# Sample attention that begins with the sliding branch, in a decoder step on one core

## What is computed

```python
o_cmp = softmax(q . kcmp) . vcmp                   # compressed blocks, 127 of them
idx   = top_k(importance of 33 blocks of 64, 16)   # 2048 past tokens and the new one
o_sel = softmax(q . k[idx blocks]) . v[idx blocks] # branch "sel", paged cache
o_win = softmax(q . k[last 512]) . v[last 512]     # branch "win", own cache
o     = g0 * o_cmp + g1 * o_sel + g2 * o_win
o_mem = softmax(qm . kmem) . vmem                  # branch "mem", 256 memory tokens
```

## Time and profile before

| | us |
|---|---|
| median of the runs | 1694.38 |
| the profiled execution, whole | 1689.1 |
| its span | 1687.2 |
| PE busy | 1472.1 (87%) |
| DVE busy | 880.0 (52%) |
| ACT busy | 374.7 (22%) |
| POOL busy | 82.0 (5%) |
| sample attention, within the span | 805 to 950 |

### The profile page before, as it was taken

The page is one execution under the profiler, slowest core; times in us unless marked ns, Lnnn a source line. Parts: engine busy times, 40 slices in busy tenths (PEclk is TensorE's granted clock), DMA queues, the critical chain, the costliest instruction groups (busy, mean ns, idle before and its releaser), DMA issues. The chain is left out here.

```text
span 1687.2 us, 27010 instructions
## 1 busy us (share of the span) xinstructions
PE 1472.1 (87%) x11343; PEld 1348.7 (80%) x11343; DVE 880.0 (52%) x1598; ACT 374.7 (22%) x874; POOL 82.0 (5%) x76
## 2 busy tenths in 40 slices
PE   6999899879878788988556567999989999999998
PEld 5778789879877677867344447999979999999998
DVE  3554257658434556654233264445654746555563
ACT  3543033223314344544122100010003101000000
POOL 0000001100011111110000000000000000000000
PEclk8999999989958798988678658999989999999999
DMA  9231125142401000000754342332341233233231
GB/s 342 87 131 59 50 79 179 51 175 79 132 10 51 0 1 1 1 1 8 302 204 156 97 149 77 92 96 77 99 164 38 75 101 100 79 97 99 75 101 51
DMA packets 115649, 159.03 MB, mean 94 GB/s; under 512 B 6040, under 2 KB 106840, under 8 KB 112779
## 3 DMA queue, kind: packets, MB, share of 16 engines
q1 hardware_dynamic: 111886, 122.76, 22.7%
q0 software_dynamic: 2304, 33.56, 4.9%
q10 hardware_dynamic: 1348, 1.12, 0.2%
HBM read 145.04 MB, written 16.66 MB: 96 GB/s over the span
## 5 line engine op out<-in xcount | busy, mean ns | idle before, releaser
L329 PE MATMUL ps<-uH,wh 128*128 128x260 f32 x576 | 165.5, 287 | 21.3 <-DVE wl L300 12.4
L298 DVE CAST wh<-wt 128x2048 fp32r<-128x2048 f32 (+1 forms) x75 | 85.7, 1143 | 128.7 <-PE ps L329 101.0
L329 PE MATMUL ps<-hH,wh 128*128 128x260 f32 x512 | 145.6, 284 | 2.6 <-DVE hT L300 2.6
L329 PE MATMUL ps<-mergedH,wh 128*128 128x260 f32 x512 | 145.5, 284 | 0.0
L329 PE MATMUL ps<-hH,wl 128*128 128x260 f32 x512 | 145.5, 284 | 0.0
L329 PE MATMUL ps<-hT,wh 128*128 128x260 f32 x512 | 144.8, 283 | 0.0
L329 PE MATMUL ps<-mergedH,wl 128*128 128x260 f32 x512 | 144.6, 282 | 0.0
L329 PE MATMUL ps<-mergedT,wh 128*128 128x260 f32 x512 | 144.6, 282 | 0.0
L456 PE MATMUL ps<-XT,w 128*128 128x256 f32 (+1 forms) x512 | 125.7, 387 | 6.3 <-DVE XT L519 6.0
L329 PEld LDWEIGHTS ps<-uH,wh 128*128 128x128 f32 x576 | 110.6, 192 | 21.6 <-issue 12.5
L300 DVE TENSOR_TENSOR wl<-wt,wh 128x2048 fp32r<-128x2048 f32 (+1 forms) x58 | 120.2, 2072 | 2.0
(11 more groups left out here) (517 smaller groups left out, 3427.3 us busy)
## 6 DMA issues: line engine op xcount, KB each, us to landing
wt<-in_w_ff SPq DMA_DIRECT2D x32, 1024.0 KB, 5.3
wt<-in_w_in SPq DMA_DIRECT2D x27, 1024.0 KB, 5.4
ring<-in_cache_mem_kv SPq DMA_DIRECT2D x4, 2048.0 KB, 25.1
w<-in_cmp_w SPq DMA_DIRECT2D x8, 512.0 KB, 7.8
ring<-in_cache_win_kv SPq DMA_DIRECT2D x2, 2048.0 KB, 19.5
wt<-in_w_out SPq DMA_DIRECT2D x4, 1024.0 KB, 6.1
out_s_win<-in_cache_win_kv SPq DMA_DIRECT2D x1, 4088.0 KB
scratch_uhigh<-uH SPq DMA_DIRECT2D x1, 2080.0 KB
```

The source lines that it names most:

```text
L298: dve.tensor_copy(high, x).then_inc(high_sem, 1)
L329: ins = pe.matmul(out, lhsT(i, c), rhs(j, c), start=(first and c == 0 and k == 0), stop=(last and c == chunks - 1 and k == 2))
```

## The change

The first group's jobs now run in the order win, sel, mem; the second group keeps sel, win, mem. Two pieces are loaded during the prompt mixers instead of one. SP loads the window piece of group 0 into w1's place as soon as the MLP has read it. POOL gathers the first selected piece into the place of graw, at the key `delta_key(3, 2.5)`, behind the transposes of graw in the last chunk; graw's place thereby becomes slot 1 of the ring. The load of a piece by SP is moved into a helper, `fetch_piece`, and the count for which PE waits on `masked` is now that of the jobs so far which have a new token.

```diff
-        self.ring_filled = 1
+        self.ring_filled = 2
-        self.ring = [self.view("w1", [P, PAGES * 256], F32)]
+        self.ring = [self.view("w1", [P, PAGES * 256], F32), self.view("graw", [P, PAGES * 256], F32)]
+        self.fetched_ahead = self.sem("e_fetched0")
...
-                yield 42
-                pool.wait_ge(self.hid_ready, hid0 + 2)
-                self.gather_piece(pool, 0, 0)
+                yield self.delta_key(TT - 1, 2.5)
+                self.d_pe.wait(pool, "tv", TT - 1)
+                self.d_dve.wait(pool, "sc", TT - 1)
+                self.gather_piece(pool, 0, 1)
...
+                sp.wait_ge(self.hid_ready, hid0 + 2)
+                self.fetch_piece(sp, "win", 0, self.ring[0]).then_inc(self.fetched_ahead, 16)
...
-                  "memhl", "qmT", "kmT", "mem_kv", "graw", *self.d_names)
+                  "memhl", "qmT", "kmT", "mem_kv", *self.d_names)
+        at, _ = self.taken.pop("graw")
+        self.taken["ring1"] = (at, at + PAGES * 256)
...
-        jobs = [(br, r) for r in range(R4) for br in ("sel", "win", "mem")]
+        jobs = [(br, r) for r in range(R4) for br in (("sel", "win", "mem") if r else ("win", "sel", "mem"))]
...
-        gathered, fetched = self.filled, [S(f"e_fetched{k}") for k in range(RING)]
+        gathered, fetched = self.filled, [self.fetched_ahead] + [S(f"e_fetched{k}") for k in range(1, RING)]
...
-                    pe.wait_ge(masked, 2 * r + (br == "win") + 1)
+                    pe.wait_ge(masked, sum(x != "mem" for x, _ in jobs[0:n + 1]))
...
-                    if what == "sel":
+                    if what == "sel" or k < self.ring_filled:
...
+                    self.fetch_piece(sp, what, r, slot(k)).then_inc(fetched[k % RING], 16)
...
+    def fetch_piece(self, sp, what, r, slot):
+        if what == "win":
+            src = self.I["cache_win_kv"][4 * r:4 * r + 4].rearrange("b (t p) v g d -> p (b t) (v g d)", p=P)
+        else:
+            src = self.I["cache_mem_kv"][4 * r:4 * r + 4, :, 0 if what == "memk" else 1].rearrange("b (t p) h d -> p (b t) (h d)", p=P)
+        return sp.dma_start(slot.rearrange("p (a c) -> p a c", a=src.shape[1]), src)
```

## The result

Timed side by side with the kernel before, the changed kernel takes 1693.76 us (median of 22 runs, 1688.6 to 1703.3) against 1686.68 us (22 runs, 1680.4 to 1696.3): a ratio of 1.0044, with a 95% interval of 1.0028 to 1.0059. That is 7.4 us slower (4.7 to 10.0). It is slower, as forecast, and the 5.7 us forecast lie inside that interval. The forecast time, 1700.1, does not hold, nor did its range of 1695.3 to 1703.6 contain the measured one: it was counted from the 1694.38 us of the three runs then shown, and these turned out to be near the slow end of what the kernel before takes. The 22 runs include these three; the other 19 have a median of 1685.45.

What follows compares the result with a forecast made beforehand. Two gather landings (828.24, 887.26) were taken to set the sample attention stage's time. Release 7.8 us later, then 2.1 less to the last landing: 1694.38 + 5.7 = 1700.1 us; range 1695.3 to 1703.6 including rivals A and B.

Steps and rivals of the forecast that it cites:

- The absolute time: Whole kernel: 1694.38 us, the median of the runs then shown, plus 5.7 for the longer stage, giving 1700.1 us.
- The third gather: First round of sample attention: the last queued gather is used 1.0 us later, behind mem's rows; bounds 3.9 earlier, 3.8 later.
- Rival A: Stage's start: SP's head start is a row count, so the last gather comes 3.8 us later; whole +8.5, 1702.9; chance 0.10.
- From sel's keys to the release: Group 0, end of sel's keys to end of sel's values: 26.8 us instead of 19.96, about 6.8 more.
- three waits read in the old rows: Between sel's keys and values: waits on DVE and ACT stay as before; sel's softmax 3.1 us late, mem's key copies behind it.
- The upper bound of 28.5: Sel's keys to the end of its values: 28.5 us if all mem blocks and scores run at the slow clock.
- From the release to the last landing: Second round, end of sel's values to use of the last gathered piece: 22.3 us, 2.1 less than 24.35.
- rival B: Second round: gathers come undisturbed, last piece used at 889.5; stage +2.2 us, 1696.6; chance 0.11.
- rival C: Both rounds: gathers go ahead of SP's rows, last landing at 884.6; 2.7 us faster, 1691.7; chance 0.07.
- The sum: Whole stage: sel's slots released 7.8 us later, then 2.1 less to the last landing; 5.7 us longer.
- win's keys as hidden in the first wait: Stage's start: win's blocks, score and softmax run from 813.5 while PE and DVE wait for gathers.
- The preload: Prompt mixers: loading win's piece ahead and moving the first gather cost nothing; 0.98 us once if POOL's idle cover were gone.

Runs made afterwards that it cites:

- order part alone: Changed kernel without gathering a selected piece into graw's place, leaving four gathers at the stage's start; ratio 1.0082 against the kernel before, stage +14.3 us.
- the freed buffer alone: Kernel before, old job order, with two selected pieces gathered ahead, into w1's and graw's places; ratio 0.9977, stage 5.8 us shorter.
- both loads held: Changed kernel, SP's mem load of group 0 and win load of group 1 waiting for their round's last gather; ratio 1.0005 against the kernel before.
- the graw part with both loads held: Old job order, two selected pieces gathered ahead, SP's win loads of both groups waiting for the round's last gather; ratio 0.9934 against the kernel before.
- win of group 1 held: Changed kernel, SP issuing group 1's window load only once that group's last selected piece has landed; ratio 1.0011 against the kernel before.
- sel's values first: Changed kernel, group 0's sel probabilities and values placed ahead of mem's keys on all engines; ratio 0.9986 against the kernel before.

## Why the prediction was right or wrong

*The absolute time: wrong.* The step that failed is "1694.38 + 5.7", and in it the first term. Three runs within 0.7 us of each other looked like the level of the kernel before. Over 22 runs it is 1686.68, 7.7 us less; with it the same sum gives 1692.4, 1.4 us from the measured 1693.76. The range gave room to the terms of the change alone and none to this one. In one kernel the time goes with the clock that TensorE was granted over the run: the changed kernel took 1688.6 at a mean of 0.908, 1693.7 at 0.905 and 1703.3 at 0.899, the kernel before 1681.3 at 0.912 and 1696.3 at 0.902. Why three runs in a row lay so close together and so high is not shown; their own clock is not on record. The profiled execution, 5.3 us below the three runs, was a sign that they were high; it should have widened the range downwards. Counted from that execution, the prediction had 1694.8, and the profiled execution of the changed kernel took 1693.7.

*The third gather: +1.0 forecast, +1.4 and +1.3 measured* in the two profiles of the changed kernel, and +0.6 in two others that start alike (used 23.03 and 23.04 us after POOL's first gather, before 22.41). The turns row by row are there: in three microseconds of the first round (815 to 818) each queue moved 81 packets, with 0.17 MB on SP's queue, where the earlier trace rows have 0.08:

```profile
q0 software_dynamic: 81, 1.07, 83.0%
q1 hardware_dynamic: 81, 0.17, 14.2%
q10 hardware_dynamic: 81, 0.04, 4.6%
```

*Rival A, a head start counted in rows: wrong.* The first gather packet comes 4.0 to 4.7 us after POOL's issue in both kernels (before 805.83 and 810.0 to 810.5, after 806.48 and 810.5 to 811.0), though SP's rows were twice as large and so half as many (96 from 810.0 to 810.5, where the earlier trace rows have 187 in half a microsecond). What ran ahead of the gathers was thus not a fixed count of rows; whether it is a time or a number of bytes, these two cannot tell.

*From sel's keys to the release: 26.8 forecast, 26.17 measured* (19.96 before). This is the term that makes the loss, and it came from three waits read in the old rows: the fourth block of mem's keys was forecast 11.75 us behind sel's keys and ran 11.77 behind (856.15). One sum in it was wrong: 17.6 and 1.9 are 19.5 and not 19.2, so that the term should have been 27.1 and the whole +6.0; the scores ended at 19.1. The upper bound of 28.5 had named the scores at the slow clock (0.50), and this happened: in the order part alone and in the two runs that hold win of group 1 in the new order, mem's scores took 3.64 us at 0.50 or 0.51 and the term was 27.9 to 28.1, though the instructions before them are the same. Why the two profiles of the changed kernel escaped it is not shown.

*From the release to the last landing: 22.3 forecast, 21.8 measured*, and with SP held 18.8 and 19.1. So the competition is real, 3 us of it, and rival B (the second round undisturbed by itself) and rival C (both rounds undisturbed by themselves) did not happen; C made by hand gives -1.4 us of stage instead of its -2.7.

*The sum: +5.7 forecast, +4.6 and +4.4 of stage, +7.4 and +7.1 by the ratios.* It counts win's keys as hidden in the first wait, and they were: blocks and scores ran from 814.15 to 821.2, and the block of the third gather came at 830.31. The preload cost nothing that shows: POOL's gather for graw stands at 714.43 with 16 us idle behind it, and win's block at 814.15 waits for no load.

## What to carry to other kernels

In a ring of buffers, a job moved ahead moves the release of another one's slots back; before reordering, look for the next load that reuses them and where it lands, since here PE did 5.6 us more of its work in the first wait (8.92 instead of 3.32) and the stage became 4.5 us longer. A job moved ahead can also take the place of a load that the others wait for. Of two queues that share the DMA engines, the one that nobody waits for can be held back until the other's transfer has landed: two such waits on SP took 4.3 us off the stage in the old order and 6.0 in the new one, where the freed buffer alone took 5.8. And runs that agree within 0.7 us may still share one level that others do not: state a forecast as a difference, and take the spread of the absolute time from more runs.

## What the runs showed of the hardware

POOL's gathers had their first packet 1.50 to 1.75 us after POOL's issue where none of SP's loads ran (issue at 863.25 before, at 847.65 in the changed kernel, at 809.89 and 871.96 with both loads held). Queued while SP's loads kept the engines busy, they waited about 3 us more, 4.0 to 4.7 us from POOL's issue, whether the rows ahead of them were of 1 KB (issue at 805.83 before; SP's queue had a share of 108.1% from 809 to 810) or of 2 KB (issue at 806.48 in the changed kernel; 105.6%).

Three gathers of 2 MB, from POOL's first issue to the use of the third, took 18.3 to 18.9 us with SP's loads held back (18.3 in the second round of the graw part with both loads held, 18.5 with win of group 1 held, 18.8 and 18.9 in the changed kernel with both loads held). They took 21.4 to 22.4 beside 1 KB rows (22.4 in the first round before, 21.5 and 21.4 in the second round of the two profiles of the changed kernel) and 23.0 to 23.8 beside 2 KB rows (23.8 and 23.7 in the first round of these two, 23.0 with win of group 1 held and with sel's values first).

In the profiles of the kernel before and of the changed one, TensorE's granted clock was 0.50 all through the waits of the first round (813.50 to 828.24 and 814.15 to 830.31). In the second round it was still 1.00 when the wait began, and fell during it. In the kernel before the wait began at 877.87, and the clock was 1.00 from 878 to 880, 0.80 from 880 to 882 and 0.50 from 882 to 884. In the changed kernel PE had worked until 871.2:

```profile
872.00:874.00 2.00, 0.00 (x0) 0.00 (x0) 0.00 (x0) 1.01 (x3) 1.55 (x2) 1.00 0.86 276
874.00:876.00 2.00, 0.00 (x0) 0.00 (x0) 0.00 (x0) 0.00 (x0) 0.33 (x1) 0.76 1.20 439
876.00:878.00 2.00, 0.00 (x0) 0.00 (x0) 0.00 (x0) 0.00 (x0) 0.00 (x0) 0.50 0.99 418
```

It came back at different moments in different executions of nearly the same instructions. In the changed kernel it was 0.50 from 852 to 861, 0.81 from 861 to 862 and 1.00 from there, and mem's scores, at 861.59, took 1.93 us; in the order part alone it was 0.50 from 856 to 869, and the same scores, at 865.48, took 3.64 us.
